# Delta rule, ends of the chunks: one order of products by rows, two PSUM banks swapped

## The reference, cut to what matters

```
state = state * w_t + (state @ -kk_t) outer (kk_t * a_t) + v_t outer k_t
y_t   = state @ r_t
```

## Time and profile before

| | us |
|---|---|
| median of 3 runs | 2179.99 (2179.44 to 2181.21) |
| the profiled execution | 2172.92 |
| its span | 2171.0 |
| PE busy | 2137.6 (98%) |
| DVE, ACT, POOL busy | 934.1, 879.4, 893.2 |
| mean granted clock of PE | 0.998 |

### The profile page before, as it was taken

The page is one execution under the profiler, slowest core; times in us unless marked ns, Lnnn a source line. Parts: engine busy times, 40 slices in busy tenths (PEclk is TensorE's granted clock), DMA queues, the critical chain, the costliest instruction groups (busy, mean ns, idle before and its releaser), DMA issues.

```text
span 2171.0 us, 30795 instructions
## 1 busy us (share of the span) xinstructions
PE 2137.6 (98%) x12606; PEld 1726.3 (80%) x12614; DVE 934.1 (43%) x1580; ACT 879.4 (41%) x1651; POOL 893.2 (41%) x688
## 2 busy tenths in 40 slices
PE   8999999999999999999999999999999999999998
PEld 6767788878888888877777888888887688888886
DVE  5231767544531021145335744443237765444322
ACT  4344631144442243243336544443244535444322
POOL 5423410025344444454232454444454345444443
PEclk9999999999999999999999999999999999999999
DMA  7222200015223223212111122222322122222321
GB/s 274 88 74 92 69 31 17 8 49 165 78 94 101 94 95 102 97 59 88 49 59 49 59 95 96 96 96 95 100 64 97 49 78 86 96 97 95 103 90 66
DMA packets 53589, 184.10 MB, mean 85 GB/s; under 512 B 5816, under 2 KB 5824, under 8 KB 53320
## 3 DMA queue, kind: packets, MB, share of 16 engines
q1 hardware_dynamic: 53448, 182.13, 25.4%
HBM read 176.84 MB, written 8.15 MB: 85 GB/s over the span
## 4 chain that ended last, share of the span: by engine, by line
PE 94%; DVE 2%; DMA 1%; ACT 1%; POOL 1%; issue 1%; SPq 0%; POOLq 0%; ACTq 0%; DVEq 0%
PE ps L332 22%; PE ps L334 22%; PE ps L333 22%; PE ps L1606 3%; PE ps L2669 2%; PE ps L2671 2%; PE ps L2670 2%; PE ps L358 1%; PE ps L352 1%; PE ps L353 1%; PE ps L1101 1%; DMA raw_units<-stream 1%; PE ps L466 1%; PE ps L1103 1%; PE ps L1102 1%; PE ps L1597 1%
## 5 line engine op out<-in xcount | busy, mean ns | idle before, releaser
L186 POOL TENSOR_TENSOR split_units<-raw_units,split_units 128x512 fp32r<-128x512 f32 x628 | 820.1, 1331 | 1117.5 <-ACT split_units L176 1117.4
L176 ACT ACTIVATE split_units<-raw_units 128x512 fp32r<-128x512 f32 x628 | 359.1, 621 | 364.0 <-PE ps L334 326.5
L332 PE MATMUL ps<-x_split,split_units 128*128 128x512 f32 x1208 | 475.1, 393 | 1.7 <-DVE work L2329 0.8
L334 PE MATMUL ps<-x_split,split_units 128*128 128x512 f32 x1208 | 470.8, 390 | 0.0
L333 PE MATMUL ps<-x_split,split_units 128*128 128x512 f32 x1208 | 470.8, 390 | 0.0
L332 PEld LDWEIGHTS ps<-x_split,split_units 128*128 128x128 f32 x1208 | 227.2, 188 | 54.1 <-issue 4.0
L333 PEld LDWEIGHTS ps<-x_split,split_units 128*128 128x128 f32 x1208 | 227.1, 188 | 48.2 <-issue 1.7
L334 PEld LDWEIGHTS ps<-x_split,split_units 128*128 128x128 f32 x1208 | 227.1, 188 | 47.8
L332 PE MATMUL ps<-hidden_split,split_units 128*128 128x512 f32 x608 | 237.3, 390 | 0.0
L334 PE MATMUL ps<-hidden_split,split_units 128*128 128x512 f32 x608 | 236.6, 389 | 0.0
L333 PE MATMUL ps<-hidden_split,split_units 128*128 128x512 f32 x608 | 236.5, 389 | 0.0
(11 more groups left out here) (483 smaller groups left out, 3259.4 us busy)
## 6 DMA issues: line engine op xcount, KB each, us to landing
raw_units<-stream SPq DMA_DIRECT2D x314, 512.0 KB, 3.7
work<-gate_rows SPq DMA_DIRECT2D x12, 256.0 KB, 2.9
bias_rows<-bias_line SPq DMA_DIRECT2D x1, 2816.0 KB
gate_rows<-work SPq DMA_DIRECT2D x10, 256.0 KB, 2.1
x<-x_t SPq DMA_DIRECT2D x4, 512.0 KB, 6.7
work<-bias_rows SPq DMA_DIRECT2D x1, 2048.0 KB
out_t<-x SPq DMA_DIRECT2D x8, 256.0 KB
vec<-vectors SPq DMA_DIRECT2D x1, 1159.5 KB, 8.2
```

The lines of the kernel that those rows point to most:

```text
L176: scalar.activation(self.split[:, u % SPLIT, 0, part], self.raw[:, u % RING, part], ACT.Copy).then_inc(self.high_done, 1)
L186: gpsimd.tensor_tensor(self.split[:, u % SPLIT, 1, part], self.raw[:, u % RING, part], self.split[:, u % SPLIT, 0, part].bitcast(F32), ALU ...
L332: TE.matmul(out, high, rhs(0, k), start=(k == 0), stop=False)
L334: ins = TE.matmul(out, low, rhs(0, k), start=False, stop=last and shift is None)
```

## The change: order and banks

PE's queue gets another order for the end of a chunk. `right_side` is cut into `right_state` (all four heads' state products, 64 rows) and `right_values` (all four value products, 128 rows). `output`'s state products become `output_state`, which now stand beside `cross`. The order is: state products of both groups, output's state products and cross of both, values of both, solve of both, output of both. Four heads' sums are open in a bank at the same time: the first product of the first two heads clears, the others add to cleared places. The right side's heads lie 128 columns apart instead of 64. `solve` writes bank 4g+2 and y goes to bank 4g+1. `token_major` of the next chunk waits for ACT_Y in place of ACT_SA; ACT's `right_side` waits for PE_G in place of DVE_CROSS; the numbers of PE_CROSS and PE_G change places.

```diff
-            PE_TURN, PE_JOIN, PE_CROSS, PE_G, PE_SA, PE_YZ = 4, 20, 22, 21, 23, 24
+            PE_TURN, PE_JOIN, PE_CROSS, PE_G, PE_SA, PE_YZ = 4, 20, 21, 22, 23, 24
...
                 def token_major(g, ch):
                     if ch:
-                        wait_act(pe, g, ch - 1, ACT_SA)
+                        wait_act(pe, g, ch - 1, ACT_Y)
...
-                def right_side(g, ch):
-                    for first in (0, 2):
-                        outs = [twice_out(slice(0, P), 4 * g + (3, 0)[i % 2], (i // 2) * HD) for i in range(4)]
-                        for i in (first, first + 1):
-                            t, r = 2 * g + i // 2, half(i)
-                            TE.matmul(outs[i], w[r, AT + t, cols(ch)], twice(z[r, t * HD:(t + 1) * HD]), start=True,
-                                      stop=False)
-                        for i in (first, first + 1):
-                            ins = TE.matmul(outs[i], n4(g, i, 2), twice(values_of(g, i)), start=False, stop=True)
+                def state_of(g, i):
+                    t, r = 2 * g + i // 2, half(i)
+                    return t, r, z[r, t * HD:(t + 1) * HD]
+                def right_out(g, i):
+                    return twice_out(slice(0, P), 4 * g + (3, 0)[i % 2], (i // 2) * P)
+                def right_state(g, ch):
+                    for i in range(4):
+                        t, r, zt = state_of(g, i)
+                        TE.matmul(right_out(g, i), w[r, AT + t, cols(ch)], twice(zt), start=(i < 2), stop=False,
+                                  skip_group_check=True)
+                def right_values(g):
+                    for i in range(4):
+                        ins = TE.matmul(right_out(g, i), n4(g, i, 2), twice(values_of(g, i)), start=False, stop=True,
+                                        skip_group_check=True)
                     ins.then_inc(pe_s[g].sem, 1)
...
-                        ins = TE.matmul(twice_out(slice(0, P), 4 * g + 1, i * HD), w[:, UF[g], i * P:(i + 1) * P],
+                        ins = TE.matmul(twice_out(slice(0, P), 4 * g + 2, i * HD), w[:, UF[g], i * P:(i + 1) * P],
...
+                def output_at(g, i):
+                    return bank(4 * g + 1, (i // 2) * P, P, half(i))
+                def output_state(g, ch):
+                    wait_dve(pe, g, ch, DVE_JOIN)
+                    for i in range(4):
+                        t, r, zt = state_of(g, i)
+                        TE.matmul(output_at(g, i), zt, w[r, R + t, cols(ch)], start=(i < 2), stop=False,
+                                  skip_group_check=True)
                 def output(g, ch):
                     wait_act(pe, g, ch, ACT_SA)
+                    taken = [w[:, XX[g], 256 + i * HD:256 + (i + 1) * HD] for i in range(4)]
+                    for i in range(4):
+                        TE.matmul(output_at(g, i), taken[i], n4(g, i, 1), start=False, stop=False,
+                                  skip_group_check=True)
+                    for i in range(4):
+                        TE.matmul(output_at(g, i), values_of(g, i), n4(g, i, 3), start=False, stop=True,
+                                  skip_group_check=True)
                     for first in (0, 2):
...
-                            TE.matmul(out, z[r, t * HD:(t + 1) * HD], w[r, R + t, cols(ch)], start=True, stop=False)
...
                     for g in range(2):
-                        right_side(g, ch)
+                        right_state(g, ch)
+                    for g in range(2):
+                        output_state(g, ch)
                         cross(g, ch)
+                    for g in range(2):
+                        right_values(g)
                     for g in range(2):
                         solve(g, ch)
...
                 def right_side(g, ch):
-                    wait_dve(act, g, ch, DVE_CROSS)
+                    wait_pe(act, g, ch, PE_G)
```

More of the change, by code:

```diff
@@ new lines, in output @@
+                    taken = [w[:, XX[g], 256 + i * HD:256 + (i + 1) * HD] for i in range(4)]
[5 more added lines that the diff above has]
+                                  skip_group_check=True)
+                    for first in (0, 2):
+                        zz = {i: bank(4 * g + 3, (i // 2) * HD, HD, half(i)) for i in (first, first + 1)}
+                        for i, out in zz.items():
+                            TE.matmul(out, w[:, BK[g], i * HD:(i + 1) * HD], taken[i], start=True, stop=False)
+                        for i, out in zz.items():
@@ L1862, in right_side @@
                 def right_side(g, ch):
-                    wait_dve(act, g, ch, DVE_CROSS)
+                    wait_pe(act, g, ch, PE_G)
                     out = w[:, XX[g], 0:256].rearrange("p (a b d) -> p a b d", a=2, b=2)
                     for b in range(2):
-                        ins = S.activation(out[:, :, b, :], bank(4 * g + (3, 0)[b], 0, P).rearrange(
-                            "p (a d) -> p a d", d=HD), ACT.Copy)
+                        ins = S.activation(out[:, :, b, :], bank(4 * g + (3, 0)[b], 0, 2 * P).rearrange(
+                            "p (a d) -> p a d", d=P)[:, :, 0:HD], ACT.Copy)
                     ins.then_inc(act_s[g].sem, 1)
@@ L1871, in taken_up @@
                     wait_pe(act, g, ch, PE_SA)
-                    S.activation(w[:, XX[g], 256:512], bank(4 * g + 1, 0, 256), ACT.Copy).then_inc(act_s[g].sem, 1)
+                    S.activation(w[:, XX[g], 256:512], bank(4 * g + 2, 0, 256), ACT.Copy).then_inc(act_s[g].sem, 1)
                 def unity(g, ch):
@@ L1880, in output @@
                     S.activation(w[:, YB + 2 * g:YB + 2 * g + 2, cols(ch)],
-                                 bank(4 * g + 2, 0, 256).rearrange("p (a t) -> p a t", a=2),
+                                 bank(4 * g + 1, 0, 256).rearrange("p (a t) -> p a t", a=2),
                                  ACT.Copy).then_inc(act_s[g].sem, 1)
```

## The result

The changed kernel took 2161.3 us (median of 4, 2159.43 to 2166.42) against 2180.45, ratio 0.9922, 95% interval [0.9911, 0.9934]. Two more sets of five runs gave 2162.16 (0.9918 [0.9903, 0.9932]) and 2164.0 (0.9935 [0.9921, 0.9949]).

A forecast was written before the change was run, and what follows sets the result against it. PE was taken to bound the kernel. Four chunk ends, each 2.7 us shorter by fewer changes of shape and a lost wait, give 10.8 us: 2180.0 - 10.8 = 2169.2 us, range 2166.2 to 2173.5.

The forecast's parts named there:

- What bounds it: Whole kernel: PE is busy 98% of the span and 94% of the chain, so only time from PE's queue counts.
- the steady steps: PE at chunk ends: 0.056 us per 64-row product instruction, 0.111 per 128*128 or cross instruction, without changes of shape.
- the prices of the changes: PE at chunk ends: each change of product shape costs 0.13 to 0.20 us, two per output round 0.30.
- What is removed: Each chunk end: changes of shape 3.26 us and a wait of 0.16, 3.42 of 13.16; products of 9.74 all stay.
- the rule on modes and tiles: Borders between output's state products and cross: changing the array corner without changing shape costs nothing; otherwise 1.6 us return.
- Waits: PE's waits on ACT's copies at solve and token_major: slacks about 0.17 to 0.18 us, and the present 0.16 wait goes.
- rival 1: Waits replace changes of shape: the three slacks are missed, PE loses 0.33 us at three places, 4.0 in all: 2173.2; chance 0.13.
- Rival 2: Sums left open across banks are dear: 0.16 us restart per head, 5.1 in all: 2174.3; chance 0.07.
- Rival 3: Granted clock falls to half at chunk ends where 64-row products stand together: slower, about 2182.2 us; chance 0.03.
- Rival 4: The merge stage's low-clock stretch goes, saving another 1.7 us: 2167.5; chance 0.09.
- the sum: Whole kernel: 10.8 us off the profiled 2172.9 gives 2162.1; carrying over the median's unexplained 7.1 gives 2169.2; chance 0.68.
- the two borders without a row of their own: Chunk-end changes 64*128 to 64*64 and 128*128 to 128*64, not occurring before: priced as the group entered, bounds 0 and 0.20.

## Why the prediction was wrong, by its own steps

- **What bounds it, the steady steps, the prices of the changes**: right. Undoing half of the change at a time gave 11.49 and 11.31, where these prices, with the overlap added after the result, gave 11.54 and 11.3. Three of four parts of the chunk end came to 0.04 us.
- **What is removed**: this step failed. "The products themselves are 9.74, and the diff leaves all of them" is true of the work and false of the time: output's state products (0.89 a chunk) ran while cross ran, and the block of both took 1.91 for 2.80. Taking steady time as a sum holds only while the products use the array one behind the other. The earlier trace rows showed it before: four instructions of L1606, in two corners, start from 307.04 on and the next of L1641, in a third, at 307.15: one step of 0.11 for all of them. I read there that the border is free, the point of the rule on modes and tiles, and not that both run at once. With 3.56 for 2.7 a chunk the forecast is 2180.0 - 14.2 = 2165.8.
- **Waits**: right, rival 1 did not come; slacks of 0.19, 0.19 and 0.16 on the prediction's terms, for 0.18, 0.18 and 0.17.
- **Rival 2** (open groups dear): no; values and solve run at 0.111 a step. **Rival 3** (clock falls in the chunk ends): no, 1.00 in all of them in every profile. Its sum was loose: 21.6 us of low clock hold 10.8 us of work, a quarter of the four chunk ends, and not half.
- **Rival 4 and the sum**: rival 4 did not come, the merge stage's low stretch is still there in the profile after (3.4 us near 446). The 7.1 us between the profile and the median, "which no view explains", were mostly the clock: the profile stood at 0.998 and the kernel before elsewhere at 0.994 on average, 4 x 1.6 = 6.4. I allowed the after kernel one stretch more or less, 1.7 us; executions of it differ by 9.9 (2156.5 to 2166.4), and medians of 4 and 5 of them by 2.7. So the range would have been too narrow below even with the overlap in it. The other, larger share of the miss, 2165.8 against 2161.3, goes with the clock: the four executions stood at 0.993, 0.997, 0.997 and 0.998, and at the 0.9944 of the kernel before the kernel after would take about 2164.7 + 0.6 x 1.6 = 2165.7. How much of that is the luck of the draw is open; the third set (2164.0) says part of it.
- A slip that moves nothing: the two borders without a row of their own are priced at 0.13 and 0.15 in the sum and come back as 0.33 in the lower end of the range; with 0.28 it is 2166.4 in place of 2166.2.

## What to carry to other kernels

When products of less than the full array are put next to each other, ask two things of each pair of neighbours: does the shape change (0.13 to 0.20 us here), and do they use different corners in the same shape? Then the shorter run can be free, if it is cut into short groups: eight instructions ahead of cross cost 0.02 us a chunk end, sixteen cost 0.60. A move that saves the first can bring the second, and once it does, the longer of the two is the one to shorten: here cross, 0.8 us a chunk end for one edit. And before a median is set against a profile, set their mean clocks side by side.

## What the runs showed of the hardware

- Matmuls did not start in the order of the queue: those of a free corner passed up to six that waited for theirs, in two kernels (2 of 8 and 10 of 16 state instructions started before the first of cross). The Trainium skill, TensorE: Matmul & The Clock Gate, Part 3, says that matmuls keep program order at start and end. The starts recorded here differ, and the measurement decides; the ends are modelled and settle nothing.
- A run in one corner goes at 0.109 us an instruction with 128 columns streamed, and with 64 it let the block of 32 instructions (state products and cross) shrink from 1.91 to 1.1 us; the weight loads (0.13 us each in both) were not the limit of the 0.109.
